# Eight samples' state update in one head of a hybrid decoder step: two products of 64 rows become one pair of 32-row tiles

## What is computed

```python
G = cumsum(log f)                                  # over the sample's 8 tokens
dS = einsum('td,tv->dv', k * exp(G_last - G), i)   # 128 x 128
S_new = exp(G_last)[:, None] * S_old + dS
o = (q * exp(G)) @ S_old + masked(q exp(G), k exp(-G)) @ i
```

## Time and profile before

| | |
|---|---|
| median of 3 runs | 2210.88 us (2209.92 to 2212.13) |
| profiled execution | 2210.85 us |
| its span, first to last instruction | 2209.3 us |
| PE busy | 2094.8 us, 95% of the span |
| DVE, ACT, POOL busy | 1047.0, 828.0, 74.1 us (47%, 37%, 3%) |
| mean granted clock of TensorE | 0.968 |
| moved by DMA | 443.86 MB, mean 201 GB/s |

### The profile page before, as it was taken

How to read it: one execution, slowest core, us unless ns; L and a number is a source line. 1 busy time by engine, 2 the same in 40 slices (tenths; PEclk the granted TensorE clock), 3 DMA queues, 4 the chain that set the end, 5 groups by cost and what they waited for, 6 DMA issues and landing times.

```text
span 2209.3 us, 38997 instructions
## 1 busy us (share of the span) xinstructions
PE 2094.8 (95%) x14722; PEld 1951.7 (88%) x14722; DVE 1047.0 (47%) x1323; ACT 828.0 (37%) x1066; POOL 74.1 (3%) x118
## 2 busy tenths in 40 slices
PE   7999999899998999979999799999999999999994
PEld 7999878777777878759999699999999999999994
DVE  6443544435454544536544644444444444445445
ACT  5323343425334342434433433333333333345342
POOL 1001001010101001000000000000000000000000
PEclk9999999999999999979999899999999999999997
DMA  7767677877868777875644244444444444444431
GB/s 258 159 232 266 254 292 268 305 285 277 314 225 318 249 286 275 306 260 186 243 154 144 77 149 147 151 151 144 150 151 144 145 146 145 162 149 139 159 123 48
DMA packets 123844, 443.86 MB, mean 201 GB/s; under 512 B 14485, under 2 KB 18597, under 8 KB 123728
## 3 DMA queue, kind: packets, MB, share of 16 engines
q1 hardware_dynamic: 113872, 403.78, 51.7%
q0 software_dynamic: 9920, 39.38, 6.3%
HBM read 423.19 MB, written 22.54 MB: 202 GB/s over the span
## 4 chain that ended last, share of the span: by engine, by line
PE 92%; DVE 3%; ACT 2%; DMA 2%; issue 1%; SPq 0%; ACTq 0%; DVEq 0%
PE ps L385 23%; PE ps L386 22%; PE ps L387 22%; PE ps L1417 5%; PE ps L1415 5%; PE ps L1416 5%; PE ps L801 3%; PE ps L835 2%; DMA raw<-w_in 1%; PE ps L635 1%; PE ps L810 1%; PE ps L629 0%; PE ps L631 0%; PE ps L578 0%; PE ps L608 0%
## 5 line engine op out<-in xcount | busy, mean ns | idle before, releaser
L344 DVE TENSOR_TENSOR w_lo<-raw,w_hi 128x1024 fp32r<-128x1024 f32 x416 | 504.3, 1222 | 598.9 <-ACT w_hi L339 293.7
L385 PE MATMUL ps<-x_hi,w_hi 128*128 128x320 f32 x1408 | 455.4, 323 | 51.3 <-DVE stage L428 41.5
L385 PE MATMUL ps<-h_hi,w_hi 128*128 128x320 f32 x1408 | 436.1, 310 | 11.2 <-DVE h_lo L1355 10.6
L386 PE MATMUL ps<-x_hi,w_lo 128*128 128x320 f32 x1408 | 442.4, 314 | 0.0
L387 PE MATMUL ps<-x_lo,w_hi 128*128 128x320 f32 x1408 | 441.8, 314 | 0.0
L386 PE MATMUL ps<-h_hi,w_lo 128*128 128x320 f32 x1408 | 435.1, 309 | 0.0
L387 PE MATMUL ps<-h_lo,w_hi 128*128 128x320 f32 x1408 | 435.1, 309 | 0.0
L339 ACT ACTIVATE w_hi<-raw 128x1024 fp32r<-128x1024 f32 x240 | 250.3, 1056 | 417.5 <-PE ps L387 417.5
L385 PEld LDWEIGHTS ps<-x_hi,w_hi 128*128 128x128 f32 x1408 | 272.0, 193 | 108.8 <-issue 61.6
L385 PEld LDWEIGHTS ps<-h_hi,w_hi 128*128 128x128 f32 x1408 | 264.7, 188 | 13.2 <-ACT stage L1291 11.5
L386 PEld LDWEIGHTS ps<-x_hi,w_lo 128*128 128x128 f32 x1408 | 272.3, 193 | 0.0
(11 more groups left out here) (264 smaller groups left out, 2327.8 us busy)
## 6 DMA issues: line engine op xcount, KB each, us to landing
raw<-w_in SPq DMA_DIRECT2D x176, 512.0 KB, 7.0
raw<-w_up SPq DMA_DIRECT2D x176, 512.0 KB, 3.3
raw<-ck SPq DMA_DIRECT2D x128, 512.0 KB, 6.0
raw<-cv SPq DMA_DIRECT2D x128, 512.0 KB, 5.8
raw<-w_dn SPq DMA_DIRECT2D x88, 512.0 KB, 3.3
raw<-w_out SPq DMA_DIRECT2D x32, 512.0 KB, 4.3
uT<-stage POOLq DMA_DIRECT2D x14, 640.0 KB, 3.8
raw<-w_hg SPq DMA_DIRECT2D x16, 512.0 KB, 4.9
```

The costliest lines, as they stand in the source:

```text
L344: dve.tensor_tensor(w_lo[half][:, :], raw[slot][:, :], w_hi[half][:, :].bitcast(F32), ALU.subtract).then_inc(lo_ready, 1)
L385: pe.matmul(out, wh[:, c, m, :], xh(c), start=first, stop=False)
L386: pe.matmul(out, wl[:, c, m, :], xh(c), start=False, stop=False)
```

## The change

The table `own` gets 4 columns in place of 8 and a one in column (token // 8) mod 4: column block j of `i_own` now holds the rows of sample j in its first 32 partitions and those of sample 4 + j in the other 32. DVE makes it once, at q = 6. PE multiplies both halves at q = 8, as two matmuls of 32 rows by 512 columns, the first on partitions 0 to 31 into bank 6, the second on partitions 32 to 63 into bank 5. L621 and the second `own_part` are gone, with DVE's wait between them. All eight state updates move to q = 10.

```diff
-        own = sb("own", [CHUNK, NB], F32, at_in)
+        own = sb("own", [CHUNK, NB // 2], F32, at_in)
-        h_pe = Steps(sem("h_pe"), "scores vk i_t kd_t a ds pd_t pv ds_s0 o ds_s1", 1)
+        h_pe = Steps(sem("h_pe"), "scores vk i_t kd_t a ds pd_t pv o ds_s", 1)
-        h_vec = Steps(sem("h_vec"), "fg kin s max nmax G Gd qkd rc rcl pd2 pd own0 aT st1 st2 st3 st4 own1 s_new0 o s_new1", 1)
+        h_vec = Steps(sem("h_vec"), "fg kin s max nmax G Gd qkd rc rcl pd2 pd own aT st1 st2 st3 st4 o s_new", 1)
 # vec_head
-            def own_part(b):
-                return dve.tensor_tensor(
-                    i_own[:, :, :], i_tok[:, 4:5, :].broadcast_to([CHUNK, NB // 2, DV]),
-                    own[:, 4 * b:4 * b + 4].unsqueeze(2).broadcast_to([CHUNK, NB // 2, DV]), ALU.mult)
-
             def new_state(b, bank):
                 for k in range(4 * b, 4 * b + 4):
                     last = SEQ + NQ * k + NQ - 1
                     ins = dve.scalar_tensor_tensor(s0[:, k, :], s0[:, k, :], eG[:, last:last + 1],
                                                    ps[:, bank, k % 4 * DV:(k % 4 + 1) * DV], ALU.mult, ALU.add)
-                h_vec.done(ins, f"s_new{b}")
+                return ins
             if q == 6:
                 dve.wait_ge(h_act.sem, h_act.at(h, "i_tok"))
-                h_vec.done(own_part(0), "own0")
+                h_vec.done(dve.tensor_tensor(
+                    i_own[:, :, :], i_tok[:, 4:5, :].broadcast_to([CHUNK, NB // 2, DV]),
+                    own[:, :].unsqueeze(2).broadcast_to([CHUNK, NB // 2, DV]), ALU.mult), "own")
 # q == 7, behind the chain of states
-                dve.wait_ge(h_pe.sem, h_pe.at(h, "ds_s0"))
-                h_vec.done(own_part(1), "own1")
             if q == 9:
                 dve.wait_ge(h_pe.sem, h_pe.at(h, "o"))
-                new_state(0, 6)
                 h_vec.done(dve.tensor_copy(o_hg[:, bass.ds(h, 1), :].rearrange("p a t -> p (a t)"),
                                            ps[:, 4, 0:T]), "o")
             if q == 10:
-                dve.wait_ge(h_pe.sem, h_pe.at(h, "ds_s1"))
-                new_state(1, 5)
+                dve.wait_ge(h_pe.sem, h_pe.at(h, "ds_s"))
+                new_state(0, 6)
+                h_vec.done(new_state(1, 5), "s_new")
 # pe_head
-                h_pe.done(pe.matmul(ps[:, 6, :], kd_tok[:, 4, :], i_own[:, :, :], start=True, stop=True), "ds_s0")
             if q == 8:
                 pe.wait_ge(h_act.sem, h_act.at(h, "o_att"))
-                pe.wait_ge(h_vec.sem, h_vec.at(h, "own1"))
-                h_pe.done(pe.matmul(ps[:, 5, :], kd_tok[:, 4, :], i_own[:, :, :], start=True, stop=True), "ds_s1")
+                pe.wait_ge(h_vec.sem, h_vec.at(h, "own"))
+                for b in range(2):
+                    t = slice(32 * b, 32 * b + 32)
+                    ins = pe.matmul(ps[:, 6 - b, :], kd_tok[t, 4, :], i_own[t, :, :], start=True, stop=True)
+                h_pe.done(ins, "ds_s")
 # pool_head
-            pool.wait_ge(h_vec.sem, h_vec.at(h, "s_new1"))
+            pool.wait_ge(h_vec.sem, h_vec.at(h, "s_new"))
 # the host's table
-        "c_own": (i[:, None] // NQ == np.arange(NB)[None, :]).astype(np.float32),
+        "c_own": (i[:, None] // NQ % 4 == np.arange(NB // 2)[None, :]).astype(np.float32),
```

## The result

| | before | changed |
|---|---|---|
| median (22 runs each) | 2210.95 us | 2215.38 us |
| lowest to highest | 2207.67 to 2216.18 | 2209.87 to 2222.41 |
| span of the profiled execution | 2209.3 | 2215.2 |
| mean granted clock | 0.968 | 0.960 |

The ratio of the changed kernel to the one before is 1.002, 95% interval 1.0014 to 1.0027: about 4.4 us slower, where 2196 us (14.8 us faster) was forecast. The interval does not reach 1, so this small loss is no noise; single executions of either kernel scatter by several microseconds.

A forecast was written before the change was run, and what follows sets the result against it. The prediction took PE, holding 92% of the chain that ended last, as the bound. Work of -9.1 + 0 + 1.1 = -8.0 us and clock of -6.8 us made -14.8, so 2196 us, range 2190 to 2202.

The forecast's parts named there:

- PE, q = 6 (-9.1 us): Removing L621 lets PE's next granule start 1.14 us earlier a head, -9.1 us over eight heads, all on the path.
- the pair (0): At q = 8 two 32-row matmuls replace one of 64 rows; run side by side they cost 0.
- DVE (0): Four updates, 1.12 us, move to q = 10; 2.55 us of slack before the turn absorbs them, cost 0.
- the last round (+1.1): Without granules D, PE waits for the exponential there, so the moved updates cost 1.1 us on the path.
- DVE's 50.6 us of waiting: DVE's eight waits for L621 are idle time of an engine 47% busy; removing them was costed at nothing.
- The clock (-6.8 us): Two fewer middle falls (-3.3) and seven round starts at 1.6 us (-3.5); bounds about -25 to +6 us.
- the sign: At round starts, PE's return to the scores was to take 5.3 to 5.6 us if the forecast held.
- one of the prediction's own signs of being wrong: Rounds shorter by less than 1 us on average would show the forecast wrong.
- The clock gives nothing: Rival: clock falls stay or get dearer, giving 2202.8 us, or 2209 at the dear bound; chance 0.17.
- A new fall behind the pair: Rival: the clock falls at q = 8, 2.7 us a head, giving 2224.5 us; chance 0.05.
- Series: Rival: the pair's matmuls at q = 8 run one after the other, +7.4 us, giving 2203.5 us; chance 0.12.
- late loads: Rival: POOL's later traffic delays loads while DMA is full, +4.8 us, giving 2200.9 us; chance 0.07.

The follow-up runs named there:

- cut_before: Kernel before with only the first sample product (L621) and DVE's wait on it taken out, so four samples' new states are wrong: 2215.06 us.
- fill512: Changed kernel with one idle fp32 matmul of 64 rows by 512 columns put back where the removed one stood: 2211.87 us.
- fill256: Changed kernel with one idle fp32 matmul of 256 columns put back where the removed one stood: 2212.24 us.
- split_after: Changed kernel with the last group of page scores moved inside the head's output, between the 64-column and 8-column products: 2200.24 us.

## Why the prediction was wrong

**PE, q = 6 (-9.1 us) and the pair (0):** right, 1.23 us a head where 1.14 were forecast, and 1.06 us for the pair against 1.05. The scores had been the right row to price a pair of tiles. The Trainium skill's rule (TensorE: Matmul & The Clock Gate, Part 3: Packing small matmuls), matmuls starting in program order, was read there as making the pair longer by half a matmul. The 1.06 us speak against that reading, as the 0.86 of the earlier trace rows did: in head 3 the pair's four records start at 571.66, 571.67, 572.19 and 572.20, so the tiles take turns record by record. The rule itself, of whole matmuls, is not contradicted by this.

**DVE (0) and the last round (+1.1):** right. No round with granules D waits for the exponential; the last waits 1.0 us more. That DVE's 50.6 us of waiting were worth nothing was right too.

**The clock (-6.8 us)** is the step that failed, in sign and in bound. The prediction counted a fall as one thing of 1.64 us that is there or is not, and so could bound the loss at one more fall in head 0 and the dearest starts, +6. The runs showed a third case: a middle fall twice as long, 10.2 us from output to product without one (head 0 of the kernel before: its output begins at 260.36, its product at 270.58), 11.85 with the short one, 13.42 with the deep one. In head 0 it cost 3.2 us where there was none, in the next six 1.6 us more each: about 12.6 us. The starts gave no cheap end either: the seven stretches from PE's return to the scores are 5.8 to 6.5 us long in the changed kernel, 42.3 us together against 40.0 before, where 5.3 to 5.6 had been named as the sign. From the samples' product to the next scores, which takes in these stretches, both kernels come to 342 us in seven rounds, so the starts neither gave nor took. Work was -9.8 us at PE and +1.0 in the last round; so for the 4.4 us measured the clock's term must be about +13 us, where -6.8 was taken.

The reading of the earlier trace rows behind that term was loose as well. Its two stretches are not the same place of the round: that of head 0 begins 4.4 us ahead of the output, that of head 3 1.3 us behind it. The conclusion holds, since from 261.60 to 271.60 head 0 has 1.00 too. That two of the six middle falls would go had no row to say so. One of the prediction's own signs of being wrong came true with the time: the six rounds were not 1 us shorter but 0.2 us longer.

The reason given for the choice was also wrong: that the two rounds "before the pattern had settled" were cheap, and that a shorter round would unsettle the pattern. The opposite is seen. Rounds of some kernels with different work settle near the same length: 98.95 us on average in the changed kernel, 99.0 in cut_before (520.91 to 619.91; its seven run from 98.2 to 99.8), 98.98 in fill512:

```profile
518.61 0.50 PE L582 MATMUL ps<-mk,mq 64*128 64x128 f32 x4
...
617.59 0.50 PE L582 MATMUL ps<-mk,mq 64*128 64x128 f32 x4
```

fill512 does at least 1.05 us more a round than the changed kernel, and its rounds are as long. For these kernels a saved microsecond was paid to the clock, and an added one was had for nothing. It is no law: fill256's rounds are uneven, and those of split_after lie between 95.2 and 100.0 us. Why the rounds settle at this length where they do is not shown. The Trainium skill (same page, Part 1: The HAM clock gate) says that the monitor runs free and does not start over with the kernel. The trace agrees in so far as the same instructions found the clock in another state from one kernel to the next, and single runs of one kernel scatter by 8.5 us (before), 12.5 (changed) and 16.7 (fill256).

**The rivals.** "The clock gives nothing" named the right place, with 0.17, and its dear end, 2209 us, was too near. "A new fall behind the pair" did not come in the changed kernel. It did when the 8-column products were moved next to the pair, but also with the single product in the pair's place. Its reason, that a pair of 32-row tiles uses less of the array, was no reason: together the two tiles have the 64 rows of the product that they replace. Series and late loads did not come.

## What to carry to other kernels

Where the granted clock of a repeated round is below 1.00, read what a saving on PE is worth only after asking where the slow stretches will lie, and bound them by a longer fall, not only by one more. Put an idle matmul where the removed one stood, and take the old one out alone, before blaming the new code: these two runs told cause from position here. Fix the clock first (idle matmuls through a stall, small products broken up by dense ones); the same change lost 4.4 us without, and gained 13.7 us with the idle matmuls in the stall.

## What the runs showed of the hardware that was not expected

The clock can fall while PE is busy without a gap (PE busy 10.00 of 10.00 us at 0.66), in or just behind 64- and 8-column fp32 products that take 4.6 us at full clock. It need not: the same products left it at 1.00 in head 0 of the kernel before. With page scores between them (32-column tiles, 512 columns wide) it still fell in four of seven heads of the changed kernel, in two of them for so long that output to pair took 14.9 us, and in one of seven heads of the kernel before. Twenty 128-column fp32 matmuls in the stall held it at 1.00, and cost nothing that the stall did not cover: PE's next granule began 5.62 us behind the turn back (594.93 to 600.55), and 5.69 without them (308.13 to 313.82, first round of the kernel before). Two fp32 tiles of 32 rows by 512 columns into two banks take 1.06 us, as one of 64 rows does.
